# Turning the expert table: units of four panels loaded in four pieces, whole rows stored per turn

## The reference

```
h      = gelu(x . u[e])          for each of the 128 picks e of a token
out    = sum over picks of gate * h * v[e]
```

## Time and profile before

| | |
|---|---|
| three runs, median (lowest to highest) | 2460.21 us (2450.05 to 2463.08) |
| the profiled execution | 2449.04 us, span 2447.3 us |
| TensorE busy | 2081.8 us (85%) |
| VectorE busy | 1566.5 us (64%) |
| DMA | 648.10 MB, mean 265 GB/s |
| turns (L199) | 128, 153.8 us busy, 159.3 us idle before them |

### The profile page before, as it was taken

How to read it: one execution, slowest core, us unless ns; L and a number is a source line. 1 busy time by engine, 2 the same in 40 slices (tenths; PEclk the granted TensorE clock), 3 DMA queues, 4 the chain that set the end, 5 groups by cost and what they waited for, 6 DMA issues and landing times. The chain is left out here.

```text
span 2447.3 us, 24440 instructions
## 1 busy us (share of the span) xinstructions
PE 2081.8 (85%) x8036; PEld 1398.3 (57%) x8036; DVE 1566.5 (64%) x3423; ACT 482.7 (20%) x1053; POOL 835.0 (34%) x637
## 2 busy tenths in 40 slices
PE   5998759876979998999998988888866659989977
PEld 4775748754835895565555555555522347734445
DVE  4567554445999985666666666666777776436752
ACT  3344022212211330000000000000000122335541
POOL 3420014423301005666555454544566233310002
PEclk8988569988989998999999999999988879999999
DMA  6988869994856459999999999999999522200001
GB/s 223 340 262 214 225 214 306 338 282 169 277 179 245 164 196 385 403 403 403 403 402 402 402 402 402 402 404 404 402 401 400 209 74 69 61 22 1 1 35 69
DMA packets 254077, 648.10 MB, mean 265 GB/s; under 512 B 20864, under 2 KB 119296, under 8 KB 252672
## 3 DMA queue, kind: packets, MB, share of 16 engines
q1 hardware_dynamic: 168560, 335.60, 39.8%
q0 software_dynamic: 73728, 268.47, 27.9%
q10 hardware_dynamic: 11664, 42.47, 5.2%
HBM read 560.48 MB, written 85.98 MB: 264 GB/s over the span
## 5 line engine op out<-in xcount | busy, mean ns | idle before, releaser
L1534 PE MATMUL ps<-arena 128*128 128x512 f32 x1024 | 519.4, 655 | 142.8 <-DVE arena L1391 101.8
L1402 DVE CUSTOM_DVE_ANT_0 arena<-arena 128x1024 bf16<-128x1024 f32 x256 | 313.1, 1224 | 250.9 <-DMA arena<-u_rows,expert 139.2
L1523 PE MATMUL ps<-rows_n,arena 128*128 128x256 f32 x2048 | 465.4, 380 | 0.0
L1523 PEld LDWEIGHTS ps<-rows_n,arena 128*128 128x128 f32 x2048 | 387.5, 191 | 96.4 <-issue 50.0
L1534 PEld LDWEIGHTS ps<-arena 128*128 128x128 f32 x1024 | 207.6, 209 | 398.9 <-issue 262.5
L1273 POOL DMA_INDIRECT arena<-u_rows,expert x256 | 289.3, 1130 | 312.1 <-DMA gates<-arena 169.2
L1273 POOL DMA_INDIRECT arena<-in_v,expert x192 | 207.8, 1082 | 323.1 <-DVE arena L1423 296.0
L199 DVE STREAM_TRANSPOSE tdst<-tsrc 128x1024 f32<-128x1024 f32 x128 | 153.8, 1226 | 159.3 <-DMA tsrc<-in_u 158.8
L1423 DVE SCALAR_TENSOR_TENSOR arena<-arena,wt 128x1024 f32<-128x1024 f32 x192 | 246.0, 1281 | 0.5
L1500 ACT ACTIVATE ge<-dots 128x2 f32<-128x2 f32 x128 | 26.0, 203 | 908.5 <-DVE dots L1402 908.5
L244 POOL TENSOR_TENSOR in_wlo<-in_raw,in_whi 128x1024 fp32r<-128x1024 f32 x45 | 115.4, 2567 | 231.7 <-ACT in_whi L240 231.7
(11 more groups left out here) (383 smaller groups left out, 3005.3 us busy)
## 6 DMA issues: line engine op xcount, KB each, us to landing
tsrc<-in_u SPq DMA_DIRECT2D x64, 1024.0 KB, 9.0
u_rows<-tdst SPq DMA_DIRECT2D x256, 256.0 KB, 5.4
arena<-in_u SPq DMA_DIRECT2D x128, 512.0 KB, 10.4
arena<-in_v SPq DMA_DIRECT2D x128, 512.0 KB, 11.5
in_raw<-in_panels ACTq DMA_DIRECT2D x37, 512.0 KB, 4.1
gates<-arena SPq DMA_DIRECT2D x8, 2048.0 KB, 8.7
arena<-gates SPq DMA_DIRECT2D x32, 512.0 KB, 18.7
mg_raw<-in_panels ACTq DMA_DIRECT2D x28, 512.0 KB, 6.1
```

The lines of the kernel that those rows point to most:

```text
L1402: nc.vector.tensor_tensor_reduce(out=junk[:, n % 2], in0=u_slot[n % NU], in1=hrows[:, n // NPICK], scale=1.0, scalar=0.0, op0=ALU.mult, op ...
L1523: mm = nc.tensor.matmul(ps[:, j % 2, 0:TD], ud[:, j % RJ, k], rows_n2[:, 0, k], start=k == 0, stop=k == KD - 1)
L1534: mm = nc.tensor.matmul(ps[:, 4 + 2 * t + c], park[:, j % NPK, t * P:(t + 1) * P], vd[:, j % RJ, c * T:(c + 1) * T], start=j == 0, stop=j ...
```

## The change

The turner works in units of four panels. A unit is one contiguous 2 MB of the input, laid over all 128 partitions (partition 32a + l gets rows 4l to 4l+3 of panel a), and loaded with four DMAs of 512 KB (`pieces` q), each with 4 KB per partition. tsrc holds two units (32 KB per partition, before 16). Turn x = 4n + b takes the experts 32b to 32b+31 of all four panels; its output holds, in each partition, one whole row of u_rows. tdst holds two turns (8 KB per partition, before 16). Each turn is stored with one DMA of 512 KB, 4 KB per partition. A turn waits for the store of the turn two before it; a unit waits for its four pieces. The pieces of unit n+2 are issued after turns 4n+3 (two), 4n+4 and 4n+5 (one each).

Rows of u_rows now lie in another order, so the index of a row is computed from the expert by swapping two fields of two bits each (`u_row`), with five more instructions of VectorE (four of them behind a wait on the one before) in each of the two `finish` that write experts. The copy of the token rows writes with another permutation. In the merge the turns are spread over all groups but the last two. To make room, hf and hq share a tile and the probabilities of window attention take 256 columns instead of 512. The counts TURNS stay.

```diff
-        def load(self, sp):
-            j, n = self.n_load, len(self.src) * self.unit
-            if j - self.first >= n:
-                sp.wait_ge(self.turned, j - n + self.unit)
-            k = (j - self.first) // self.unit % len(self.src)
-            sp.dma_start(self.src[k], io["u"][j:j + self.unit].rearrange("j p k e -> p j k e")).then_inc(self.loaded[k], 16)
-            self.n_load += self.unit
+        def load(self, sp, pieces):
+
+            for x in range(pieces):
+                n, q = divmod(self.n_load, 4)
+                if q == 0 and n >= 2:
+                    sp.wait_ge(self.turned, 4 * (n - 1))
+                if n < EXP_N // 4:
+                    sp.dma_start(tsrc[:, n % 2, q], io["u"][4 * n:4 * n + 4].rearrange("a (l q) k e -> (a l) q (k e)", q=4)[:, q]
+                                 ).then_inc(self.loaded[n % 2], 16)
+                    self.n_load += 1
 
         def fill(self, sp):
...
+            self.load(sp, 8 - min(8, self.n_load))
 
         def after(self, sp):
-            j = self.n_store
-            k = (j - self.first) // self.unit % len(self.dst)
-            sp.wait_ge(self.turned, j + self.unit)
-            rows = u_rows[j * EXP_N:(j + self.unit) * EXP_N]
-            for q in range(4):
-                sp.dma_start(rows[:, q * 256:(q + 1) * 256].rearrange("(b l) d -> l b d", l=32),
-                             self.dst[k][32 * q:32 * q + 32].rearrange("l j b k d -> l (j b) (k d)")).then_inc(self.stored[k], 16)
-            self.stores[k] += 1
-            self.n_store += self.unit
-            if self.n_load < self.end:
-                self.load(sp)
+            x = self.n_store
+            sp.wait_ge(self.turned, x + 1)
+            sp.dma_start(u_rows[P * x:P * x + P], tdst[:, x % 2]).then_inc(self.stored[x % 2], 16)
+            self.n_store += 1
+            if x >= 3:
+                self.load(sp, (1, 1, 0, 2)[x % 4])
...
         def turn(self, v):
...
+            x = self.n_turn
+            n, b = divmod(x, 4)
+            if b == 0:
+                v.wait_ge(self.loaded[n % 2], 64 * (n // 2 + 1))
+            if x >= 2:
+                v.wait_ge(self.stored[x % 2], 16 * (x // 2))
+            blocks = tsrc[:, n % 2].rearrange("p q (k b l) -> p (q k) b l", k=KD, b=4)
+            nc.vector.transpose(tdst[:, x % 2].rearrange("p (x l) -> p x l", l=32), blocks[:, :, b]).then_inc(self.turned, 1)
             self.n_turn += 1
...
-    tsrc = sbr(turn_st, "tsrc", [P, 2, 2, KD, P])
-    tdst = sbr(turn_st, "tdst", [P, 2, 2, 4, KD, 32])
+    tsrc = sbr(turn_st, "tsrc", [P, 2, 4, KD * P])
+    tdst = sbr(turn_st, "tdst", [P, 2, D])
...
-            prob = sb(st, name + "_prob", [P, NPB, T])
+            prob = sb(st, name + "_prob", [P, NPB, max(j["n"] for j in jobs)])
...
-    hf = sb(b1h, "hf", [P, HG, T])
+    hq = hf = sb(b1h, "hq", [P, HG, T])
...
-        places = [4 * m for m in range(KD) for x in range(3)] + [4 * KD + m for m in range(KD - 2)]
-        panel_stage("mg", PAN["merge"], with_side(specs, lambda u, s: sum(turns_after(x, range(len(places)), T_MG)
-                                                                          for x, y in enumerate(places) if y == u)),
-                    weights=mg_weights)
+        mms = list(range(5 * KD - 2))
+        panel_stage("mg", PAN["merge"], with_side(specs, lambda u, s: turns_after(u, mms, T_MG)), weights=mg_weights)
...
+                    e, (swap_a, swap_b) = expert[:, t - ND], (u_row[:, NG + a] for a in range(2))
+                    step(nc.vector.scalar_tensor_tensor(out=e, in0=ptile[:, x % 2, 1], scalar=float(EXP_N), in1=ptile[:, x % 2, 0],
+                                                        op0=ALU.mult, op1=ALU.add))
+
+                    nc.vector.tensor_scalar(swap_a, e, 2, 0x60, ALU.logical_shift_right, ALU.bitwise_and)
+                    nc.vector.tensor_scalar(swap_b, e, 2, 0x180, ALU.logical_shift_left, ALU.bitwise_and)
+                    step(nc.vector.tensor_scalar(u_row[:, t - ND], e, 0x3e1f, None, ALU.bitwise_and))
+                    step(nc.vector.tensor_tensor(swap_a, swap_a, swap_b, ALU.bitwise_or))
+                    nc.vector.tensor_tensor(u_row[:, t - ND], u_row[:, t - ND], swap_a, ALU.bitwise_or).then_inc(S["expert"], 1)
...
-                    ins = nc.scalar.activation(hrows[:, t].rearrange("p (q k l) -> p k q l", q=4, l=32)[:, 4 * c:4 * c + 4],
-                                               ps[:, 4 + 2 * t + c].rearrange("p (k q l) -> p k q l", k=4, l=32), ACT.Copy)
+                    ins = nc.scalar.activation(hrows[:, t].rearrange("p (q k l) -> p k l q", q=4, l=32)[:, 4 * c:4 * c + 4],
+                                               ps[:, 4 + 2 * t + c].rearrange("p (k l q) -> p k l q", k=4, l=32), ACT.Copy)
```

More of the change, by code:

```diff
@@ L148, in __init__ @@
         def __init__(self):
-            self.loaded = [top.enter_context(nc.semaphore(f"tn_loaded{k}")) for k in range(3)]
-            self.stored = [top.enter_context(nc.semaphore(f"tn_stored{k}")) for k in range(3)]
+            self.loaded = [top.enter_context(nc.semaphore(f"tn_loaded{k}")) for k in range(2)]
+            self.stored = [top.enter_context(nc.semaphore(f"tn_stored{k}")) for k in range(2)]
             self.turned = top.enter_context(nc.semaphore("tn_turned"))
             self.n_load, self.n_turn, self.n_store = 0, 0, 0
-            self.loads, self.stores, self.filled = [0] * 3, [0] * 3, [0] * 3
@@ L180, in after @@
-            self.stores[k] += 1
-            self.n_store += self.unit
-            if self.n_load < self.end:
-                self.load(sp)
+            x = self.n_store
[4 more added lines that the diff above has]
+                self.load(sp, (1, 1, 0, 2)[x % 4])
         def drain(self, sp):
-            for k in range(3):
-                if self.stores[k]:
-                    sp.wait_ge(self.stored[k], 64 * self.stores[k])
+            for k in range(2):
+                sp.wait_ge(self.stored[k], 16 * (EXP_N // 2))
@@ L290, in _ @@
                         also(sp)
-                    for x in range(turns // turner.unit):
+                    for x in range(turns):
                         turner.after(sp)
@@ L422, in _ @@
                     side_load(sp)
-                for x in range(sum(s["kind"] == "U" for s in specs) // turner.unit):
+                for x in range(sum(s["kind"] == "U" for s in specs)):
                     turner.after(sp)
@@ L846, in _ @@
         def _(sp):
-            for x in range(T_HG // turner.unit):
+            for x in range(T_HG):
                 turner.after(sp)
@@ L1270, in _, with fetch @@
         def _(pool):
-            def fetch(dst, table, n, landed):
+            def fetch(dst, table, rows, n, landed):
                 t, k = divmod(n, NPICK)
```

16 lines of the change are left out of this document (4 added, 12 removed).

## The result

The changed kernel takes 2432.62 us (median of nine runs, 2427.3 to 2441.25), the kernel before beside it 2452.43 us (nine runs, 2441.07 to 2463.08). The ratio is 0.9926, 95% interval 0.9903 to 0.9949: 18 us less. The forecast was 2431, and that the time lies so near it is luck: it was taken off the 2460.21 us of three runs, and the median of the kernel before over nine runs is 8 us lower. As a difference the forecast was 29.5 us, and 18 (by the ratio) to 20 (by the medians) came, about halfway to the 8.5 us of the rival "the wait is only exchanged". The direction and the range held, the size did not.

The account below looks back on a forecast made before the run. DMA at 400 to 404 GB/s bounds slices 15 to 30; earlier, about 40 us of waits reach the end. Terms -14 - 17 - 1 + 2.5 = -29.5 us, from 2460.2, give 2431; range 2403 to 2453.

Parts of the forecast that it names:

- the wait is only exchanged: Rival, 14%: store landings in the full merge replace load waits; gain 0 there, 10 us in the recurrence: -8.5 us, 2452.
- The bound: Turns, all stages: late loads are the cost; pieces issued earlier and 2.7 us of DMA per turn bring load waits to zero.
- what is late next: Turns with two-deep tdst: each waits for the store two before; 2.3, 2.9 or at worst 4.0 us a turn.
- In1: Stage in1: VectorE's 53.5 us of load waits are covered by TensorE, so only about 1 us is gained.
- Recurrence: Recurrence: TensorE becomes the bound, its waits of 16.8 us shrink to some 3; gain 14 us, bounds 0 and 25.
- the 0.4 + 4.2 of the sum: Recurrence turns: 0.4 us of issue plus 4.2 us of store landing with a load piece ahead, giving 2.9 us a turn.
- the 66 to 72 named: Sign that the forecast is right: the recurrence takes 66 to 72 us, with waits on stores.
- the rival with the higher clock: Rival, 20%: TensorE, kept fed, has the higher clock; recurrence -24 us, merge -20, in all -42.5: 2418.
- Merge: Merge: turns at 2.9 us just fit, so TensorE's gap is 7 us instead of 23.8; gain 17 us, bounds 0 and 21.
- The sum by DMA time: Merge, first part: 105 us of DMA for turns plus 31 for weights, less 4 MB, against TensorE's 132: nearly full.
- The index: Ranking to gates: five more VectorE instructions per `finish`, some 1.25 us, twice; costs 2.5 us, bounds 1.5 and 4.
- The rule weighed: Loads: the skill page asks 1 MiB per DMA; unoverlapped, 6.4 us of DMA per turn and a far slower kernel.

Follow-up runs that it names:

- the old places: The changed kernel with the merge's turns back in bunches behind the first gate of each m, where they were before, against the changed kernel: 2431.21 us, ratio 0.9906.

## Why the prediction was right, and where not

**The bound, right.** With pieces issued further ahead and one store a turn the load waits went to zero, as said. Stores and loads were changed at once, so what each did for that is not shown. The store waits named as "what is late next" are what came, 137.7 us of them. In1 is covered by TensorE again (124.15 of 127 us), with 53.5 us of waits, now for stores.

**Recurrence, right within 3 us.** -14 forecast, -11.4 measured with the norm. The landing there is 4.6 us by the trace, and it holds the issue; that is the 0.4 + 4.2 of the sum, so the bound of 2.9 us a turn was right. The turns came 3.3 us apart all the same: only 10 of the 20 waited for a store, and VectorE has other work between them. TensorE's waits for the states fell by 7.6 us, not by 13.8. The 75 us of this window lie 3 over the upper end of the 66 to 72 named. The clock stayed at 0.57 in the mean, so the rival with the higher clock in this stage had nothing. The -11.4 lie nearer to the -10 of "the wait is only exchanged" than to my -14.

**Merge, wrong, and this is the step that failed.** "So 2.3, 2.9 and at worst 4.0 us a turn; I take 2.9 in the recurrence", and the same 2.9 for the merge. It measured 4.2. What was mis-sized is L, the landing of a store: I took 0.4 + 4.2, from eight stores alone on an idle queue (2.2 us), a second 256 KB and one load piece; in the merge's traffic it is 6.4, issue included. A shorter landing alone (half of the loads, 4.8 us) brings the gap to 5.7, a third slot to 7.2. The earlier trace rows had it: 512 KB loads landing in 6.4 us in that very stretch. I had listed it as the worst case and gave it to a rival, on the word that "a queue with less in it lands sooner". But the queue had no less in it: what the stores no longer held back, the loads filled (8.4 us to landing). The merge part of the rival "the wait is only exchanged" is what happened: landing 6.5 foreseen and 6.4 found, 4.05 a turn foreseen and 4.2 found, gap as before. (The near match of 4.05 is partly luck: it counts the issue twice, and 1.2 + 6.4 gives 3.8.) Both wrong signs named, store waits over 20 us in the merge and the gap as long as before, are there, and of the right signs DMA above 350 GB/s in full stretches is missing in the merge, with 310. So stage by stage the run was the rival that I gave 14%, not the forecast with 57%. That the whole is nearer to 2431 than to that rival's 2452 comes from 4.9 us before the recurrence that neither foresaw (both had 1), an index stretch that grew by 1.1 for 2.5, and the higher time that both were taken off.

**Why the old stores were slow, not shown.** I put the 190 GB/s of the earlier trace rows down to 32 partitions and 1 KB pieces. In the changed kernel neither does it alone: pieces of 1 KB in a single DMA cost no time that shows, and at four DMAs a turn 32 partitions against 128 differ by 4 us, with overlapping intervals. Four DMAs against one cost 24 to 28 (2459.16 and 2463.26 against 2435.54; the kernel before had the same median beside both, within 0.5 us). But the number does not explain the kernel before either. It had two a turn, as the form with two has that keeps 0.9924. Its SyncE took a median of 0.79 us for each of them, where that form takes 0.43, and so was at it for 3.0 to 4.5 us a unit before it could issue the next load. No kernel was run with the old stores and the new loads, or the other way round, so how the gain divides between the two is open.

**The sum by DMA time, wrong in kind.** 2.7 us of DMA per turn and "nearly full" was a budget of the engines. The window shows 310 GB/s at a busy share of 0.87, and a third slot draws 357 at 0.92. The queue had room; VectorE was not allowed to use it. The reading that led there was too wide as well: 60 to 99% busy at 214 to 340 GB/s holds for the first nine slices of the earlier trace rows, to 550 us; the next three, which reach to 734 us, have 169, 277 and 179 GB/s with the engines 40 to 90% busy.

**Small terms.** The index is right in size, 1.19 us each for 1.25, by two errors that cancel: the sum names three waits of 0.1 us but leaves them out (it would be 1.5), and the first three steps start 0.13 us apart where 0.22 was paid for each. Three of the five steps wait for the one before, not four. The stretch as a whole grew by just 1.1 and not by 2.4 or more; part of that is the ranking itself, which between the two expert steps took 54.1 us in the kernel before and 54.0 in the changed one with an index in it. The start and wa gained 4.9 us where I had 1. At in1's barrier SyncE has nothing left to issue: its last issue before the barrier starts at 161.08 and takes 0.48 us, and TensorE waits 1.0 us there, where before SyncE was busy until 165.04 and TensorE waited 2.3. Wa gained 2.95 us, but kernels of both forms lie between 71.0 and 74.0 in it. No turn waits in wa in any of them. What goes with its length is TensorE's clock: the granted clock is 0.75 there before and 0.78 after, and the stage has 27 to 34 us at the lower level in the kernels with 71.0 to 72.0 us, 37 to 41 in those with 72.3 to 74.0. That the change brought the higher clock is not shown. The spread of the turns in the merge was put at nothing, and by the trace of the old places cost 5 us of gap: it brings one turn more ahead of the last product.

**The rule weighed, half right.** No stage became slower with loads of 512 KB rather than 1 MB, and the far slower kernel that the rule would have made did not come, as the earlier trace rows said; 1 MB loads in the changed kernel were not run. The row did answer the rule as I had put it, that of the time on the engines. But the fixed part which is hidden on a full queue is not hidden from someone who waits for that one DMA: the shortest store here landed in 2.6 us, the median in 4.7. By the fit in the Trainium skill, "DMA: Bandwidth & Descriptors", section "Anatomy of one DMA", which is given there for DMAs issued by GpSimd, 512 KB take an estimated 3.2 us for a DMA by itself; that is between the shortest and the median landing here, and half of what the merge shows. The same page of the Trainium skill, section "Rules for kernel authors", says that two transfers to disjoint halves of the partitions serialize and asks for one over all 128. The time of the kernel with four stores of 32 partitions fits with that, 28 us slower than with one; but the kernel with four over all partitions is nearly as slow, so no run here shows that it is the split of the partitions that costs.

## What to carry to other kernels

With an output tile of two buffers, two steps take at least one step and one landing, counted from the start of the issue. So before a buffer is cut from four deep to two, take the landing from the busiest stretch in which it will run, not from an idle queue, and compare it with the interval that the stage needs. If it does not fit, one more slot in a tile that is dead by then (19 us here), or work moved behind the product that gates the next engine (12 us), is worth more than the pieces of a transfer (no time that shows) or one DMA for two (3.4 us, not clear of noise). Four DMAs for one buffer of 512 KB did cost 24 to 28 us.

## What the runs showed of the hardware

- The landing of one 512 KB store, from the start of its issue and with nothing of its own changed: 2.6 us at the shortest, 4.6 in the recurrence (276 GB/s), 6.4 in the merge (310), 4.8 there with half the load bytes (297), 7.5 with a third slot (357).
- The busy share of the DMA engines is not their load. In the merge it was 0.93 at 306 GB/s before, 0.87 at 310 after, 0.92 at 357 with a third slot.
- SyncE issues one 512 KB store in 0.33 us (median), one 512 KB load in 0.56 and up to 1.9, four stores of 128 KB in 1.9 to 2.0 (medians of the stages). In the kernel before four stores of 256 KB took 3.0 to 4.5.
- The final attention, the same code in all, took about 251 us in the profiles of the kernel before and of six others and 259 to 260 in those of the changed kernel, its repeat and three more; two lie at 253. The first 104 us of it, and then the first 20, in the kernel before and then in the changed one:

```profile
2196.00:2300.00 104.00, 102.95 (x420) 46.92 (x421) 72.68 (x286) 55.34 (x166) 0.00 (x0) 1.00 0.00 1
...
2196.10:2216.10 20.00, 19.70 (x81) 9.09 (x81) 13.94 (x58) 11.70 (x34) 0.00 (x0) 1.00 0.01 2
```

```profile
2180.00:2284.00 104.00, 102.89 (x391) 45.88 (x392) 67.51 (x265) 52.23 (x156) 0.00 (x0) 0.92 0.00 1
...
2180.60:2200.60 20.00, 19.92 (x48) 7.72 (x49) 9.29 (x37) 7.93 (x22) 0.00 (x0) 0.57 0.00 1
```

TensorE is busy to the same share in both, and gets through 420 matmuls at the full granted clock and 391 at 0.92. The difference is one stretch: in the changed kernel the clock falls to its lower level (1.2 GHz) 1.6 us into the stage and stays there for 17 us, though TensorE is busy for 19.92 of the first 20 us, while in the kernel before it stays at the higher one (2.4 GHz). All five long kernels show that stretch at that place, and no other does. Both lengths occur with the changed form (the third slot has 251.2 us), so it is no effect of the change as such; why the clock falls in some and not in others is open. It is why the spans of single profiles (7.9 us apart) say less than the medians (19.8 apart), and medians of four or five runs can hold some of it too.
